# First 49 blocks of the expert product with 512-column passes, their halves added by GpSimd, and the choice turned five blocks sooner

## The reference

```python
qh = (xt @ w_peer_q).reshape(T, PEER_HEADS, 2, PEER_HALF)
s = jnp.einsum('thpd,hpnd->thpn', qh, sub_keys)          # 2 x 128 scores for each of 8 heads
sv, si = lax.top_k(s, PEER_TOPK)
cand = sv[:, :, 0, :, None] + sv[:, :, 1, None, :]
best, pick = lax.top_k(cand, PEER_TOPK)
gates = jax.nn.softmax(best, axis=-1)
...
hval = jnp.einsum('cd,chkd->chk', xc, expert_u[ic])
a = gc * jax.nn.gelu(hval, approximate=False)
out = jnp.einsum('chk,chkd->cd', a, expert_v[ic])
```

## Time and profile before

| | |
|---|---|
| median of 3 runs | 1404.54 us (1404.23 to 1405.07) |
| the profiled execution | 1404.01 us, of which the span is 1402.2 us |
| TensorE busy | 1388.1 us, 99% of the span |
| VectorE busy | 987.7 us, 70% |
| ScalarE busy | 809.0 us, 58% |
| GpSimd busy | 41.8 us, 3% |
| granted clock of TensorE, mean | 0.999 |

### The profile page before, as it was taken

How to read it: one execution, slowest core, us unless ns; L and a number is a source line. 1 busy time by engine, 2 the same in 40 slices (tenths; PEclk the granted TensorE clock), 3 DMA queues, 4 the chain that set the end, 5 groups by cost and what they waited for, 6 DMA issues and landing times.

```text
span 1402.2 us, 22369 instructions
## 1 busy us (share of the span) xinstructions
PE 1388.1 (99%) x8604; PEld 1244.6 (89%) x8604; DVE 987.7 (70%) x1790; ACT 809.0 (58%) x1533; POOL 41.8 (3%) x49
## 2 busy tenths in 40 slices
PE   8999999999999999999999999999999999999998
PEld 6998888888898888899999999999988888888886
DVE  7877766666786567789997777778766555555555
ACT  6875555554665554554445877776655444555543
POOL 3002030000000000000000000000000000000000
PEclk9999999999999999999999999999999999999999
DMA  6533476665454446545556444444456656555562
GB/s 228 181 121 128 135 217 191 180 191 185 159 159 135 149 153 235 184 151 183 170 175 208 139 150 136 136 146 141 147 165 217 224 194 195 195 194 193 191 193 100
DMA packets 67568, 240.95 MB, mean 172 GB/s; under 512 B 8453, under 2 KB 8837, under 8 KB 67078
## 3 DMA queue, kind: packets, MB, share of 16 engines
q1 hardware_dynamic: 67462, 239.52, 52.8%
HBM read 237.39 MB, written 2.10 MB: 171 GB/s over the span
## 4 chain that ended last, share of the span: by engine, by line
PE 87%; DVE 8%; ACT 2%; issue 1%; DMA 0%; POOL 0%; SPq 0%; POOLq 0%; ACTq 0%; DVEq 0%
PE bank L2131 85%; DVE wl L542 3%; PE bank L2229 1%; PE bank L2217 1%; ACT wh L1527 1%; DVE eq L1370 1%; DVE eq L1373 1%; DVE ij L1376 1%; DVE St L732 0%; ACT kdz L1533 0%; DMA x<-in_x 0%; DVE pos__227 L1307 0%; DVE h L567 0%; DVE x L1041 0%; DVE sgt L1039 0%
## 5 line engine op out<-in xcount | busy, mean ns | idle before, releaser
L542 DVE TENSOR_TENSOR wl<-raw,wh 128x1024 fp32r<-128x1024 f32 x429 | 523.2, 1226 | 263.8 <-ACT wh L1527 262.8
L2131 PE MATMUL bank<-hTb,wh 128*128 128x256 f32 (+2 forms) x2864 | 596.4, 302 | 0.9 <-DVE wl L542 0.9
L1527 ACT ACTIVATE wh<-raw 128x1024 fp32r<-128x1024 f32 x429 | 448.6, 1054 | 232.4 <-PE bank L2131 229.3
L2131 PEld LDWEIGHTS bank<-hTb,wh 128*128 128x128 f32 (+1 forms) x2864 | 456.5, 191 | 17.2 <-issue 1.4
L2131 PE MATMUL bank<-hTb,wl 128*128 128x256 f32 (+1 forms) x1640 | 454.3, 282 | 0.0
L2131 PE MATMUL bank<-wh,hTb 128*128 128x512 f32 x1488 | 426.3, 393 | 1.2 <-DVE hTb L576 0.8
L2131 PEld LDWEIGHTS bank<-wh,hTb 128*128 128x128 f32 x1488 | 279.7, 188 | 60.1 <-DVE wl L542 1.5
L2131 PEld LDWEIGHTS bank<-hTb,wl 128*128 128x128 f32 (+1 forms) x1640 | 312.3, 190 | 4.5
L2131 PE MATMUL bank<-wl,hTb 128*128 128x512 f32 x744 | 244.9, 390 | 0.0
L2131 PEld LDWEIGHTS bank<-wl,hTb 128*128 128x128 f32 x744 | 140.2, 189 | 28.2
L2054 ACT ACTIVATE gates<-bank 128x256 f32<-128x256 f32 (+31 forms) x118 | 38.1, 323 | 76.7 <-PE bank L2131 76.6
(11 more groups left out here) (384 smaller groups left out, 1170.9 us busy)
## 6 DMA issues: line engine op xcount, KB each, us to landing
raw<-in_wts SPq DMA_DIRECT2D x441, 512.0 KB, 3.3
x<-in_x SPq DMA_DIRECT2D x4, 256.0 KB, 4.8
sk<-in_sk SPq DMA_DIRECT2D x1, 1024.0 KB, 6.7
spill<-x SPq DMA_DIRECT2D x1, 1024.0 KB, 7.7
x<-spill SPq DMA_DIRECT2D x1, 1024.0 KB, 6.2
out<-h SPq DMA_DIRECT2D x4, 256.0 KB, 2.1
gb<-in_g_ffn SPq DMA_DIRECT2D x1, 512.0 KB, 4.6
gb<-in_norm_mix_g SPq DMA_DIRECT2D x1, 512.0 KB
```

Source lines behind the costliest of these rows:

```text
L542: e.tensor_tensor(b[:, :], raw[u % RAW][:, :], a[:, :].bitcast(F), ALU.subtract).then_inc(S("lo"), 1)
L1527: e.activation(parts_of(u)[0][:, :], raw[u % RAW][:, :], ACT.Copy).then_inc(S("hi"), 1)
L2131: return e.matmul(o, l, r, start=first, stop=last, skip_group_check=True)
```

## The change

`NP` goes from 53 to 48. U0 to U48 are now M blocks (`n <= NP`). ScalarE copies the whole bank, both halves, to a tile `us` in SBUF (`block_out`, two buffers, which lie where `ga` lies); GpSimd adds the halves into `gates` (49 operations of 128x256); ScalarE takes the GELU from there, one block later in its stream (`early_gelu(n - 1)`). TensorE's bank is free again after the copy (`u_out`). The results of the choice are turned after U47 instead of U52, the 64 rounds begin five blocks sooner, and the last stage has 15 M blocks instead of 10. E blocks go from 118 to 64, those of the 64 rounds.

```diff
-NP, NB = 53, 5
+NP, NB = 48, 5
...
-        ga = [M(f"ga{i}", [128, 256]) for i in range(5)]
+        gaT = M("ga", [128, 5, 256])
+        ga = [gaT[:, i, :] for i in range(5)]
+
+        us = [gaT[:, 2 * i:2 * i + 2, :] for i in range(2)]
...
+            for n in range(NP + 1):
+                e.wait_ge(S("u_out"), n + 1)
+                product(gates[:, ORDER[n], :], us[n % 2][:, 0, :], us[n % 2][:, 1, :], "u_sum", ALU.add)
             norm(5)
...
-            gelu(0)
+            def block_out(n):
+
+                high(nth("U", ORDER[n]) + LOOK)
+                e.wait_ge(S("done"), nth("U", ORDER[n]) + 1)
+                if n >= 2:
+                    e.wait_ge(S("u_sum"), n - 1)
+                copy(us[n % 2].rearrange("p a t -> p (a t)"), B[2 + n % 4][:, :]).then_inc(S("u_out"), 1)
+
+            def early_gelu(n):
+                g = gates[:, ORDER[n], :]
+                e.wait_ge(S("u_sum"), n + 1)
+                e.activation(g, g, ACT.Gelu).then_inc(S("gelu"), 1)
+
+            block_out(0)
             scores_out(3)
             for n in range(1, 39):
-                gelu(n)
+                block_out(n)
+                early_gelu(n - 1)
...
             for n in range(39, NP):
-                gelu(n)
+                block_out(n)
+                early_gelu(n - 1)
+            early_gelu(NP - 1)
...
-            gelu(NP)
+            block_out(NP)
+            early_gelu(NP)
...
-                if n >= 4:
+                if 4 <= n < NP + 5:
+                    e.wait_ge(S("u_out"), n - 3)
+                elif n >= NP + 5:
                     e.wait_ge(S("gelu"), n - 3)
-                if built(n) == 256:
+                if built(n) == 256 or n <= NP:
                     unit_M(("U", ORDER[n]), B[2 + n % 4])
```

## The result

The changed kernel takes 1410.22 us (median of 6 runs, 1409.87 to 1410.69), the kernel before beside it 1404.42 (6 runs, 1404.11 to 1405.07): a ratio of 1.0041, interval 1.0028 to 1.0054. It is slower by 5.8 us, where the forecast, 1407.6, was 3.2 above this median before and the range ended at 1412.5. The profiled executions have spans of 1408.2 and 1402.2 us, 6.0 apart, both at the full clock.

A forecast was written before the change was run, and what follows sets the result against it. VectorE's chain was taken to bound the first 45 blocks. Sooner start -0.7, blocked operations +4.7, TensorE-bound blocks behind -0.6 gave +3.4 us on 1404.01, 1407.4, stated as 1407.6; range 1402.5 to 1412.5.

The forecast's parts named there:

- The bound: First 45 blocks: they end when VectorE's choice ends; its chain from U22 to U45 runs 72.46 us without a wait.
- The M form, -0.064 us a block: TensorE, 54 blocks changing form: 2.816 us each against 2.880 for E, at most 3.5 us in all.
- The chain's start, -0.7 us: VectorE's chain from U22: 1.2 us sooner by TensorE's blocks, less 0.5 for ScalarE's longer path.
- The addition, 0.72 us: GpSimd's 128x256 addition alone: 0.72 us, with bounds 0.64 and 1.28.
- The blocked operations, 11.5 x 0.41 = +4.7 us: VectorE's choice: additions block 10 operations in `at_rank` and one or two in top-16 stretches, 0.41 us each.
- The price: Each fully blocked VectorE operation loses GpSimd's duration less 0.31 us: 0.41 us, bounds 0.33 and 0.97.
- What can be blocked outside it: Top-16 stretches of VectorE's choice: one or two blocked, a `low` of 1.2 us standing among one-input operations.
- rival C: VectorE's chain: every operation is blocked, MAX8 and sums too; 25 additions in 72 us, +9.0, 1413.0 us, chance 0.15.
- Behind the choice, -0.6 us: U45 to U48 and five more last-stage blocks are TensorE-bound: 9 x 0.064 = 0.6 us gained.
- B: VectorE's chain bounds, but additions fall beside one-input work or yield: -1.3, 1402.7 us, chance 0.20.
- D: First 45 blocks: VectorE does not bind and TensorE has its whole gain: -3.5, 1400.5 us, chance 0.05.
- E: Behind the choice or in the last stage: trouble adds up to 2 us to the forecast, 1409.5 us, chance 0.07.

The follow-up runs named there:

- (7): Kernel before with 48 early blocks, first 49 blocks in M form without GpSimd's additions, one product left out of the result: 1402.64 us, ratio 0.9984.
- (6): Changed kernel with M form and GpSimd's addition only for U19 to U44, all other early blocks in the old E form: 1412.13 us, ratio 1.0051.
- (4): Changed kernel without the product of `at_rank`, four VectorE operations of 2.28 us, all additions kept: 1400.63 us, one run.
- experiment 8: Changed kernel with GpSimd copying one half instead of adding two, the other half left out: 1405.40 us, one run.
- experiment 2: Changed kernel with each of GpSimd's 49 additions made twice: 1417.76 us, one run.
- the kernel in which nothing can bite: Changed kernel with GpSimd's addition replaced by a fill of the same tile that reads nothing: 1403.39 us, ratio 0.9993.
- the mixed kernel: Changed kernel with M form and additions only for U0 to U17 and U45 to U48, old E form for U18 to U44: 1403.07 us, ratio 0.9987.

## Why the prediction was right, and where it was off

*The bound.* Right. VectorE's chain from U22 to U45 sets the end of the first 45 blocks, and TensorE's waits for `wl`, 6.6 us in nine pieces, are what was said (5 to 8 us). The M form alone brings only 1.1 us to U45 (7), the additions in that chain cost all there is (6), and with 9 us taken from the chain TensorE has its whole gain (4). The working took the lead to shrink evenly, by 0.26 us a unit. It doesn't: in `at_rank` a unit takes VectorE 3.34 us (684.54 to 687.88) and 3.88 in the changed kernel (688.30 to 692.18), and between the two stretches of `at_rank` less than TensorE's 2.82 (2.59 a unit from U31's `low` at 710.40 to U37's at 725.91, in the changed kernel). So the changed kernel's first wait comes as early as U28. The end of the chain, on which the sum rests, is the same by either count.

*The M form, -0.064 us a block.* Right: copies 2.82 us apart at the full clock.

*The chain's start, -0.7 us.* -0.53 in the changed kernel. With the GELU still out of the bank (7) U22's `low` starts at 677.07 with U1 done at 627.79, 1.04 us sooner than before on that count, forecast 1.2; so ScalarE's longer path takes back 0.51, forecast 0.5.

*The addition, 0.72 us.* 0.74 alone. The prediction's rule, that whichever starts second waits and a waiting GpSimd gets its turn between two operations of VectorE, is what the two timelines show. Of the lengths of GpSimd work the Trainium skill ("GPSIMD Engine Reference", section on elementwise cycle accounting) gives the part that grows with the elements: 0.55 us for 256 by its 2.6 cycles. No addition here was under 0.726 us, so by the trace a fixed part of some 0.18 us comes on top, and the +1.5 us for the whole change was too low.

*The blocked operations, 11.5 x 0.41 = +4.7 us.* **This is the step that was mis-sized**: 14 x 0.50 = +7.1. Its parts:
- The price. I took GpSimd's duration less 0.31 us, from the masks of the earlier trace rows. It is less 0.20, in experiment 8 at a duration of 0.40 as well as here at 0.74. That is 0.13 us on each of 13 full blocks, +1.7 us; the one partial block gives 0.36 back.
- The number in `at_rank`. Ten, as forecast: eight `low` at full price, one at a third, and a comparison.
- What can be blocked outside it, forecast 1.5, found 4, +1.0 us at the price that I had. I let only operations with two SBUF inputs count. Two of the four have one: the CAST and the COPY lost 0.42 and 0.57 us. In experiment 2 a TENSOR_SCALAR of 0.23 us lasted 0.65 and one of 0.22 lasted 0.77. The forecast named the Trainium skill's page "SBUF — State Buffer" for one-input operations outside the two-port modes. The same page of the Trainium skill (section on who interferes with whom) says that `copy`, `cast` and `tensor_scalar` can enter these modes, in which VectorE uses the port pair that it shares with GpSimd, and then contend. The traces agree: 0.85 us for the CAST instead of 0.43, 0.74 for the COPY instead of 0.17. I had read the first sentence and not the second.

*One rule for both prices.* The 0.20 and the 0.31 come of one rule that the rows show: *a blocked `low` ends 1.08 us after GpSimd does*, where it needs 1.22 alone. In the changed kernel 688.30 + 1.75 is 1.08 behind 688.97, and 696.05 + 1.40 is 1.08 behind 696.37. With the masks 182.10 + 2.08 is 1.08 behind 181.25 + 1.85, and behind experiment 8's copy 687.60 + 1.41 is 1.07 behind 687.94. It is so for all 11 blocked `low` of the changed kernel from 620 us on, 1.08 to 1.09. So the loss is the time from the operation's start to GpSimd's end, less 0.14 us, and the same 0.14 fits a blocked comparison (2.15 us behind GpSimd's end, 2.28 alone) and the COPY of 128x8 (0.03, and 0.17 alone). What differed is how long GpSimd had been at it when VectorE's operation started: by its end and its duration alone, an estimate, some 0.06 us with the additions and copies that had waited, 0.17 with the mask. 0.14 more makes 0.20 and 0.31.

*MAX8 and sums* (the TENSOR_REDUCE of `at_rank`, 2.27 us throughout). Right that they aren't touched, so rival C falls. By tile, the changed kernel:

```profile
L1306 DVE MAX8 bst<-cand x16: 251/263/275, 664.4 to 719.8; 128x8 f32<-128x112 f32 x16
...
L1314 DVE FIND_INDEX8 pos__223<-bst,s x16: 267/269/273, 670.6 to 725.7; 128x8 uint32<-128x112 f32 x16
```

Nothing in them is above 0.28 us though additions ran all through them. C's 1413.0 misses the time by 2.8 us and the forecast's 1407.6 by 2.6, on the other side, so the time alone would not have told them apart.

*Behind the choice, -0.6 us.* The spans differ by 6.0 and U45's `low` by 6.5: -0.5.

*The sum as measured:* -0.5 + 7.0 - 0.5 = +6.0 us between the two profiled executions. The prediction's own step from 1407.4 to 1407.6 adds 0.2 for an execution that it puts 0.5 under the median, and gives no reason for the rest.

*The rivals.* B (the additions miss) would have given 1402.7; the kernel in which nothing can bite gives 1403.39, so B's time was about right and its condition false. D needed a chain under 70.3 us; it was 79.5. E has no row.

What stays open: why a mask that had waited was 0.17 us under way when the `low` behind it started, and a waiting addition or copy only 0.06. No run has masks beside the chain.

## What to carry to other kernels

An engine that is nearly idle isn't free if it reads the memory that the bounding engine reads: count its instructions inside the stretch where the other has no slack, each at its duration less the 0.2 us found here, and put them elsewhere if that stretch is short (the mixed kernel keeps 22 of the 49 additions and turns +5.8 us into -1.7). A faster step on the engine that waits is worth nothing in such a stretch. And a chain that feeds another engine is a list of deliveries: before moving one, check each against the time at which it is wanted, not only the last.

## What the runs showed of the hardware that was not expected

- Two operations of VectorE in a row did not shut GpSimd out: in experiment 2 one addition came in at each border, though the operations followed without a gap (2.83, 1.75, 2.82, 1.75 us).
- What a blocked operation loses follows from GpSimd's end alone: from that end on it takes its own duration less 0.14 us, whether GpSimd added, copied or masked.
- Small one-input operations can lose several times their length: the COPY of 128x8 took 0.74 us instead of 0.17.
- Blocks are mostly whole: of 14, 13 cost between 0.42 and 0.58 us. An addition that a comparison has delayed starts at the border behind it and so hits the next `low` in full; the addition issued at 695.63, in a sum that did not hold it up, is the only one that cost a part.
